# Grouped-query attention in a two-model fp32 kernel: query products and output products inside the attention steps, and the queries' root as the scale of the exponential

## What is computed

```python
def gqa_q(a, g_q, cos, sin, rope):
    q = rms_norm_2(a.reshape(B, T, GQA_HEADS, GQA_HEAD_DIM), g_q)
    if rope:
        q = apply_rope(q, cos, sin)
    return q.reshape(B, T, GQA_KV_HEADS, GQA_GROUP, GQA_HEAD_DIM)

def gqa_mixer(hc, hl, w_in, g_q, g_k, w_out, cos, sin, need_ctx):   # need_ctx is False here
    pl = hl @ w_in
    ql = gqa_q(pl[..., :GQA_Q_W], g_q, cos, sin, True)
    kl, vl = gqa_kv(pl[..., GQA_Q_W:], g_k, cos, sin, True)
    kc, vc = gqa_kv(hc @ w_in[:, GQA_Q_W:], g_k, cos, sin, False)
    return attention(ql, concat([kc, kl]), concat([vc, vl])) @ w_out
```

## Time and profile before

| | |
|---|---|
| device time, median of 3 runs | 1780.71 us (1779.12, 1780.71, 1784.82) |
| span of the profiled execution, first to last instruction | 1781.2 us |
| mean granted TensorE clock in it | 0.986 |
| PE busy | 1684.7 us (95%) |
| DVE busy | 1225.2 us (69%) |
| ACT busy | 917.5 us (52%) |
| granted clock and GB/s, in tenths | one slice of 40 below 9, in the region of 840 to 940 us |

### The profile page before, as it was taken

The page is one execution under the profiler, slowest core; times in us unless marked ns, Lnnn a source line. Parts: engine busy times, 40 slices in busy tenths (PEclk is TensorE's granted clock), DMA queues, the critical chain, the costliest instruction groups (busy, mean ns, idle before and its releaser), DMA issues.

```text
span 1781.2 us, 25178 instructions
## 1 busy us (share of the span) xinstructions
PE 1684.7 (95%) x9916; PEld 1429.3 (80%) x9916; DVE 1225.2 (69%) x1479; ACT 917.5 (52%) x1184; POOL 0.2 (0%) x4
## 2 busy tenths in 40 slices
PE   7979999999998999999989899999999989999998
PEld 5857888988876888889765768888888867789997
DVE  6955778777875778666577359776567655677754
ACT  6475664464437665467457353331233264665552
POOL 0000000000000000000000000000000000000000
PEclk9999999999999999999989999999999999999999
DMA  7913557745651456633140216446644422145551
GB/s 252 299 49 95 163 186 258 238 152 193 201 166 49 148 189 225 213 102 121 38 136 1 67 55 211 154 134 223 221 147 157 162 70 87 39 130 188 187 181 58
DMA packets 240470, 264.75 MB, mean 149 GB/s; under 512 B 7007, under 2 KB 218978, under 8 KB 240354
## 3 DMA queue, kind: packets, MB, share of 16 engines
q1 hardware_dynamic: 238428, 258.84, 44.5%
q10 hardware_dynamic: 1926, 4.32, 0.7%
HBM read 262.08 MB, written 1.05 MB: 148 GB/s over the span
## 4 chain that ended last, share of the span: by engine, by line
PE 76%; ACT 11%; DVE 10%; issue 2%; DMA 0%; ACTq 0%; DVEq 0%
PE ps L718 75%; ACT whi L1191 2%; DVE wlo L1796 2%; ACT y L1579 1%; DVE pr L2332 1%; ACT u L1582 1%; DVE small L2321 1%; DVE y L2082 1%; ACT pr L1727 1%; PE ps L1122 1%; ACT u L1370 0%; ACT sbl L1688 0%; ACT sbe L1684 0%; ACT sbt L1682 0%; DVE rstd L1986 0%
## 5 line engine op out<-in xcount | busy, mean ns | idle before, releaser
L718 PE MATMUL ps<-u,whi 128*128 128x512 f32 (+1 forms) x3472 | 895.5, 341 | 22.8 <-DVE u L2143 5.8
L718 PEld LDWEIGHTS ps<-u,whi 128*128 128x128 f32 x3472 | 596.7, 190 | 117.5 <-issue 16.4
L718 PE MATMUL ps<-u,wlo 128*128 128x256 f32 (+1 forms) x2116 | 648.7, 307 | 0.0
L1796 DVE TENSOR_TENSOR wlo<-raw,whi 128x2048 fp32r<-128x2048 f32 (+6 forms) x212 | 454.0, 2141 | 207.4 <-ACT whi L1191 199.5
L1191 ACT ACTIVATE whi<-raw 128x2048 fp32r<-128x2048 f32 (+6 forms) x212 | 380.7, 1796 | 221.2 <-PE ps L718 202.7
L718 PEld LDWEIGHTS ps<-u,wlo 128*128 128x128 f32 x2116 | 402.2, 190 | 19.6
L718 PE MATMUL ps<-hid,whi 128*128 128x512 f32 (+1 forms) x1212 | 353.6, 363 | 0.0
L718 PE MATMUL ps<-hid,wlo 128*128 128x256 f32 (+1 forms) x864 | 261.9, 303 | 0.0
L718 PEld LDWEIGHTS ps<-hid,whi 128*128 128x128 f32 x1212 | 216.2, 189 | 40.0 <-issue 3.4
L718 PEld LDWEIGHTS ps<-hid,wlo 128*128 128x128 f32 x864 | 163.5, 189 | 7.0
L2082 DVE SCALAR_TENSOR_TENSOR y<-idle_half,cc,y 128x1024 f32<-128x1024 f32 x70 | 89.9, 1285 | 4.9
(11 more groups left out here) (264 smaller groups left out, 1628.9 us busy)
## 6 DMA issues: line engine op xcount, KB each, us to landing
raw<-in_ffn_w_up SPq DMA_DIRECT2D x44, 1024.0 KB, 5.1
raw<-in_w_ff_in SPq DMA_DIRECT2D x32, 1024.0 KB, 5.3
raw<-in_w_ff_out SPq DMA_DIRECT2D x32, 1024.0 KB, 5.0
modw<-in_w_mod SPq DMA_DIRECT2D x112, 256.0 KB, 4.1
idle_half<-in_w_mod SPq DMA_DIRECT2D x80, 256.0 KB, 3.4
raw<-in_w_in_dil SPq DMA_DIRECT2D x18, 1024.0 KB, 5.2
raw<-in_w_in_sb SPq DMA_DIRECT2D x12, 1024.0 KB, 7.9
raw<-in_w_ple_gate SPq DMA_DIRECT2D x8, 1024.0 KB, 4.9
```

What stands on the lines that cost most here:

```text
L718: return pe.matmul(out_, lhsT, rhs, start=start, stop=stop, skip_group_check=True)
L1796: nc.vector.tensor_tensor(wlo[:, s % SPLIT, 0:n], raw[:, c["r"] % RAW, 0:n], whi[:, s % SPLIT, 0:n].bitcast(F32), ALU.subtract).then_inc(* ...
```

## The change

The query job is cut in two: groups 0 and 1 stay ahead of `gqa_v`, and groups 2 and 3 (`gqa_q2`, "merged") get no phase of their own on any engine. Their products, their sums and swaps, and the first two groups of `gqa_out` are issued by hand inside the 16 attention steps. The scores' four banks become two (2 and 3), the transposes' two become one (4); the scores of unit n+1 are issued at the start of step n instead of four units ahead. The queries are no longer multiplied by their root: their sums of squares are taken for each query row (four products with `sq` as weights and 4 columns of ones), the root is a column of `small`, and it becomes the scale of the exponential (ACT) and of the negative maximum (DVE). The wait for the rotated keys ahead of query group 0 goes away, since the keys have banks of their own. `gqa_out` reads its operand from the other half of `u`.

```diff
-                linear("gqa_q", Wi, 8, pairs(0, D), S, "qg")
+                linear("gqa_q", Wi, 8, pairs(0, 512), S, "qg")
                 linear("gqa_v", Wi, 8, pairs(D + 256, 256), T2, "v", mode="V")
+                linear("gqa_q2", Wi, 8, pairs(512, 512), S, "qg")
+                phases[-1].update(merged=True, g0=2)
                 phase("softmax", what="gqa")
-                linear("gqa_out", A["gqa_w_out_2"][0], 8, pairs(0, D), S, "gated")
+                linear("gqa_out", A["gqa_w_out_2"][0], 8, pairs(0, D), S, "gated", tok0=S)
...
-            if p["kind"] != "linear" or phases[p["i"] + 1]["kind"] in ("linear", "final", "dump", "cnorm"):
+            if p["kind"] != "linear" or p.get("merged") or phases[p["i"] + 1]["kind"] in ("linear", "final", "dump", "cnorm"):
                 return [], []
...
-                    if swaps[0] >= 2:
-                        pe.wait_ge(*at("rotated", swaps[0] - (1 if q["evac"] == "qg" and g == 0 else 2)))
+                    if swaps[0] >= 2 and q["evac"] not in ("qg", "kg"):
+                        pe.wait_ge(*at("rotated", swaps[0] - 2))
...
-                            last = mm(ps[:, 6 + swaps[0] % 2, :], ones, sq[:, g % 2, :], True, True)
+                            G = g + q.get("g0", 0)
+                            if G:
+                                pe.wait_ge(*at("rstd_ready", ("head", swaps[0] - 1)))
+                            for t in range(4):
+                                last = mm(head_sums(G)[:, 4 * t:4 * t + 4], sq[:, G % 2, t * P:(t + 1) * P], ones[:, 0:4], True, True)
...
+                                if t == 1 and p["name"] == "gqa_v":
+                                    gqa_scores(p["i"] + 2, 0)
+                                    gqa_scores(p["i"] + 2, 1)
...
+            def gqa_pe(p):
+                def turn(n):
+                    pe.wait_ge(*at("weights_normed", (i, n)))
+                    if n < 1:
+                        pe.wait_ge(*at("group_read_s", ("group", value["gi"])))
+                    else:
+                        pe.wait_ge(*at("turned_copied", (i, n - 1)))
...
+                ahead = {10: (0, 1), 11: (1, 2), 12: (2, 4), 13: (4, 5), 14: (5, 6)}
+                for n in range(16):
+                    if 1 <= n < 15:
+                        gqa_scores(i, n + 1)
+                    if n < 8:
+                        query_products(query, n // 4, n % 4 * 4, n % 4 * 4 + 2)
+                    if n >= 1:
+                        attend(n - 1)
+                    if n < 8:
+                        query_products(query, n // 4, n % 4 * 4 + 2, n % 4 * 4 + 4)
+                    if n in ahead:
+                        out_ahead(out_, 0, *ahead[n])
+                    if n in (4, 8):
+                        pending.append((query, n // 4 - 1))
+                        swap_pending()
+                    turn(n)
+                attend(15)
...
+            def gqa_act(p):
+                for n in range(16):
+                    if n in (4, 8):
+                        evac(query, query["groups"][n // 4 - 1])
+                        pending.append((query, n // 4 - 1))
+                    if n in (5, 9):
+                        head_rstd_pending()
+                    if n < 15:
+                        gqa_exp(i, n + 1)
+                    copy_(n)
+                    if n in (6, 7):
+                        split_high_half(out_["groups"][1][0]["s"], n - 6)
+                    if n in (11, 12):
+                        split_high_half(out_["groups"][2][0]["s"], n - 11)
+                    if n % 2 == 1 and n >= 3:
+                        high_((n - 3) // 2)
+                high_(7)
...
+            def gqa_dve(p):
+                for n in range(16):
+                    if 1 <= n < 15:
+                        gqa_max(i, n + 1)
+                    norm_(n)
+                    if n in (5, 9):
+                        pending.append((query, n // 4 - 1))
+                        rotate_pending()
+                    if n in (7, 8):
+                        split_low_half(out_["groups"][1][0]["s"], n - 7)
+                    if n in (12, 13):
+                        split_low_half(out_["groups"][2][0]["s"], n - 12)
+                    if n % 2 == 1 and n >= 3:
+                        low_((n - 3) // 2)
+                low_(7)
...
-                    if q["evac"] in ("qg", "kg"):
+                    if q["evac"] == "kg":
                         dve.wait_ge(*at("rstd_ready", ("head", swaps[0])))
...
+                        if p["name"] == "gqa_v":
+                            gqa_max(i + 2, 0)
+                            gqa_max(i + 2, 1)
```

More of the change, by code:

```diff
@@ new lines, in out_ahead @@
+            def out_ahead(p, g, k0, k1):
+                c, i = p["groups"][g][0], p["i"] - 1
+                if k0 == 0:
+                    pe.wait_ge(*at("weights_low", c["s"]))
+                    if g == 0:
+                        pe.wait_ge(*at("rotated", query_swaps[3]))
+                    else:
+                        pe.wait_ge(*at("weights_exp", (i, 15)))
+                for k in range(k0, k1):
+                    pe.wait_ge(*at("operand_low", (i, k)))
+                    for j in range(2):
+                        w = [b[:, c["s"] % SPLIT, k * c["C"] + j * P:k * c["C"] + (j + 1) * P] for b in (whi, wlo)]
+                        bank = ps[:, base_bank(c) + j, :]
+                        mm(bank.rearrange("p (h c) -> p h c", h=2), w[0], both(p, k), k == 0, False)
+                        last = mm(bank[:, 0:S], w[1], operand(p, k, S, True), False, k == KD - 1)
+                if k1 == KD:
+                    last.then_inc(*up("weights_used", c["s"]))
@@ L982, in _ @@
                 kind, i = p["kind"], p["i"]
-                if kind not in ("linear", "cnorm"):
+                if kind not in ("linear", "cnorm") and p.get("what") != "gqa":
                     swap_pending()
-                if kind in ("stick", "softmax"):
+                if kind == "stick" or p.get("what") in ("dil", "mla"):
                     last_linear(i)
+                elif kind == "softmax":
+                    pass
                 elif kind not in ("apply", "join", "scale", "entry", "cnorm"):
@@ L1019, in _ @@
                         entry_pe(p)
-                    elif p["evac"] != "ple":
+                    elif p["evac"] != "ple" and not p.get("merged"):
                         linear_pe(p)
+                elif kind == "softmax" and p["what"] == "gqa":
+                    gqa_pe(p)
                 elif kind == "stick":
@@ L1143, in _ @@
                     M = N // heads_of
-                    ahead = dict(mla=2, dil=1, gqa=4)[p["what"]]
+                    ahead = dict(mla=2, dil=1)[p["what"]]
                     for m in range(ahead):
@@ L1147, in _ @@
                     for m in range(M):
-                        if p["what"] != "gqa" and m + ahead < M:
+                        if m + ahead < M:
                             scores(m + ahead)
@@ L1151, in _ @@
                             turn(u)
-                        if p["what"] == "gqa" and m + ahead < M:
-                            scores(m + ahead)
                         if m >= 1:
@@ L1192, in split_high, with split_high_half @@
                     *up("weights_high", s))
+            def split_high_half(s, half):
+                c = splits[s]
+                n = c["kn"] * c["C"] // 2
+                sl = slice(half * n, (half + 1) * n)
+                if half == 0:
+                    act.wait_ge(landed[c["r"] % RAW], 16 * (c["r"] // RAW + 1))
+                    act.wait_ge(*at("weights_used", s - SPLIT))
+                act.wait_ge(*own())
+                nc.scalar.activation(whi[:, s % SPLIT, sl], raw[:, c["r"] % RAW, sl], ACT.Copy).then_inc(*up("weights_high", s if half else (s, 0)))
             def hidden_high(p, g):
@@ L1518, in _ @@
                     act.wait_ge(sem, value)
+                if p.get("merged"):
+                    C.end("scalar", i)
+                    continue
                 for dst, src in p.get("loads", ()):
@@ L1710, in _ @@
                     high(HEADS // 2 - 1)
+                elif kind == "softmax" and p["what"] == "gqa":
+                    gqa_act(p)
                 elif kind == "softmax":
@@ L2298, in _ @@
                     low(HEADS // 2 - 1)
+                elif kind == "softmax" and p["what"] == "gqa":
+                    gqa_dve(p)
                 elif kind == "softmax":
```

179 lines of the change are left out of this document (156 added, 23 removed).

## The result

| | before | after |
|---|---|---|
| device time, median | 1781.78 us (4 runs, 1779.12 to 1784.82) | 1794.91 us (4 runs, 1792.95 to 1803.09) |
| ratio, 95% interval | | 1.0086 (1.0057 to 1.0114) |
| span of the profiled execution | 1781.2 us | 1791.2 us |
| mean granted clock in it | 0.986 | 0.985 |

The change made the kernel slower by 0.9%, 15 us by the ratio. To see where, the two traces are laid over each other from PE's sums of squares of the keys to the product that sums the statistics ahead of the feed-forward part, **the layer** from here on: 1459.34 to 1570.27 before, 110.9 us, and 1456.75 to 1580.06 after, 123.3 us. That is 12.4 us more. The spans differ by only 10.0, because the part ahead of the layer, whose code is the same, came out 2.6 us shorter in this execution.

A forecast was written before the change was run, and what follows sets the result against it. The prediction took PE, busy 95% of the span, as the bound. Added 19.85 us less 0.2, removed 11.4, then 2.5 and 0.3 at the exit gave +11.0, 1791.7 us; range 1787 to 1796.

The forecast's parts named there:

- later norm: Exit: DVE owes work for three output groups, its last split ends behind group 3's products, delaying the norm: +2.5 us.
- The removed stall: Ahead of query group 0's sums: the keys' own banks remove a PE gap and its slow clock, -5.7 us.
- Squares: Queries' sums of squares: four narrow fp32 products replace each wide one, 0.10 us per record, 0.2 us won.
- First transposes: Attention entry: output group 0's split on ACT and DVE delays the norm; PE stands 5.0 us, plus 2.7 of slow clock.
- n = 6 and 8: PE idles 0.5 us in step 6 and 2.05 in step 8, there for query group 3's evacuation; 1.7 slow clock follows.
- Steps 9 to 14: Fresh scores, maximum, norm and odd steps' operands outlast PE's own work: 5.8 us of PE idle time.
- The exit: After the last values: other heads of groups 0 and 1 cover head 7's operands, 0; later norm +2.5 us, dummies and clock 0.3.
- The clock: Slow clock: 2.7 us at the first transposes, 1.7 in step 8, 0.3 for dummies and exit, less 2.8 removed.
- Rival D: Gaps of steps 8 to 14 and 15 add up to more half clock, up to the feed-forward part: some 4 us more, 1796; 15%.
- A: Rival, attention entry: the split does not hold the first transposes, ACT and DVE being ahead; +3.3 us, 1784; 10%.
- C: Rival: PE's own stream decides throughout, transposes ready by 1485.7 and within each step; -7.4 us, 1773; 7%.
- B: Rival: entry stall stays, but maximum and norm overlap PE's work in steps 8 to 15 as before; +1.3 us, 1782; 8%.

The follow-up runs named there:

- e6: Kernel before, one wait weakened: query group 0's sums of squares wait for the keys' roots, not their rotation; ratio to before 0.9968.
- e1: Changed kernel, output group 0's split moved from the values' job in halves into attention steps 1 to 3; ratio to before 1.0055.
- e8: Changed kernel, ten dummy products fill PE's gap ahead of the first transposes, the wait itself stays; ratio to before 1.0095.
- e9: Changed kernel, DVE norms unit n ahead of the maximum of unit n+1 in each attention step; ratio to before 1.0098.
- e3: Changed kernel, second half split of output group 1 moved from ACT's step 7 to 9 and DVE's 8 to 10; ratio to before 1.0079.
- e4: Changed kernel, output group 2 gets banks 6 and 7 and no longer waits for group 0's evacuation; ratio to before 1.0094.
- e10: e9 with PE also taking the value products of unit n-2 in step n instead of n-1; ratio to before 1.0071.
- e13: Changed kernel, behind the attention output group 0 is finished ahead of most of group 1; ratio to before 1.0091.
- e2: Changed kernel, step n issues the scores of unit n+2 behind its value products instead of n+1 at its start; ratio to before 1.0083.
- c1: Changed kernel with the edits of e1, e3, e9 and e10 together; ratio to before 1.0022.
- c2: c1 with all half splits of output groups 1 and 2 moved to other steps in place of e3's move; ratio to before 1.0017.
- c3: c2 with e13's order of output groups added; ratio to before 1.0006.

## Why the prediction was right and wrong

The direction, the main places and the likeliest chance (slower) were right. The time was off: 15.3 us (the ratio times 1781.78) where 11.0 was said, at the upper end of the range. The interval of the ratio is wide, 10 to 20 us, and the layer in the two traces is 12.4 us longer. Term by term, in the traces:

| term | said, us | in the traces, us |
|---|---|---|
| gap ahead of the first transposes | 5.0 | 4.8 |
| slow clock behind it | 2.7 | 2.0 |
| gaps in steps 6 and 8 | 2.55 | 2.4 |
| slow clock in step 8 | 1.7 | 1.7 |
| gaps in steps 9 to 14 | 5.8 | 4.5 |
| gaps in step 15 and at the last values | 1.7 | 1.5 |
| seam, groups 0 to 2: gap and slow clock | 0 | 1.8 and 1.7 |
| later norm (gap ahead of the statistics' product) | 2.5 | 0 |
| removed from the kernel before | -11.4 | -9.8 |
| all else | 0.5 | 1.8 |
| sum | 11.05 | 12.4 |

"All else" is 0.4 for restarts, -0.2 for the squares and 0.3 for dummies and clock at the exit in the prediction, and what is neither a listed gap nor slow clock in the traces. The sum is nearer than its terms deserve: steps 9 to 14 and the removed part were both put too high and partly cancel, and the seam's 3.5 us stand against 2.5 at another place.

**The removed stall**: 5.7 said, 5.7 to 5.9 measured (e6). **Squares**: 0.10 us for each narrow record, as the row said. The Trainium skill's floor (TensorE: Matmul & The Clock Gate, Back-to-back issue gap), by which eight would take an estimated 0.2 us, is not borne out for these: 0.81 us again. **First transposes**: 5.0 said, 4.82 and 4.98 measured (gap and e1), and the cause was the named one. Its slow clock was put at 2.7, from bounds of 1.7 to 2.9, and cost 1.9 here (e1 and e8). Behind the same gap of 4.82 us it cost 1.7 in e9 and 2.6 to 2.8 in e3, e4, e10 and e13, so the bounds were right. **n = 6 and 8**: 0.5 and 2.05 said, 0.53 and 1.84 measured. The 1.7 of clock stood (3.70 us at 0.55 are 1.7 us lost).

**Steps 9 to 14**: the sum "9 1.1, 10 1.5, 11 0.35, 12 1.4, 13 0.35, 14 1.1" stands against gaps of 0.80, 1.38, none listed, 1.41, none listed and 0.90. Its pattern, even and odd, held. What the prediction had not seen is that the chain hung on two queues: with DVE's order mended the same wait appears on ACT (e9).

**The exit**: the step that failed is "the seam is filled: head 6 of group 0 and heads 0 to 6 of group 1 cover head 7's operands, 0". Head 7 is covered, but group 2 needs group 0's banks, and group 0 now ends last. PE waited 1.76 us and ran slow behind it, which lost 1.7 us of its work. "Now it ends 2.5 us behind them: +2.5 on the norm" named the right engine: in the trace DVE's last evacuation follows its split at 1577.03 without delay, but only because PE had been held before; with PE let go, the gap at the end is 3.06, 2.06 more (e4). It is one cost, which shows ahead of group 2 or behind group 3. The prediction took it as fixed; e13 shows that 3.0 us at the exit came from the order in which groups 0 and 1 are finished.

**The clock** is the second term that was mis-sized. It was 2.7 + 1.7 + 0.3 - 2.8, +1.9 us; in the layer of the two traces it is 5.4 - 3.0, +2.4, the piece behind group 2's first product being the one left out. Of the 4.3 us between 15.3 and 11.0 the traces thus show 1.4. The other 3 us are in the timed runs alone, no trace shows where, and the interval of the ratio covers them.

Their mean clocks point to more slow clock, but don't show it. The missing share of the clock times the span is 28.3 us in the mean of the four runs after the change, and 20.6 in 58 runs of the kernel before in the four later batches. That is no cost yet. The mean also counts stretches in which PE stands idle (the gap ahead of the first transposes has 0.70 in it). Also, among those 58 runs, compared within their batches, a run with 1 us more of missing clock is longer by only about 0.5 us. By that price the 7.7 us of difference are worth an estimated 3.7. The batches differ as well: the runs of before beside the result are 3.4 us slower in the mean than the 58, and their clocks are not on record. Rival D had said some 4 us more through slow clock, in the steps from 8 on. In size the 15 us are nearer to it than to the forecast. Its place was wrong in the changed kernel's trace, since steps 9 to 15 ran at 1.00; but e1's trace has just such a stretch at steps 14 and 15. Which share of the 15 us is D's stays open.

Rivals A and C (first transposes not held, PE deciding throughout) fell with the 4.82 us; B fell with the steps of 3.3 to 5.4 us after n = 7.

## What to carry to other kernels

Before filling one engine's idle time with another stage's work, write down for each in-order queue what the moved instructions now stand ahead of; here the split in front of a 0.65 us norm, the maximum in front of a norm, and an exponential in front of a copy cost more than the holes that were filled. When groups share the exit with a slower engine, finish the first group early: its evacuation chain, not the products, sets the end. And look for the smallest edit that removes the known stall; one weakened wait gave 5.7 us, and the rebuilt schedule of which it was a part took 15.

## What the runs showed that was not expected

- The same gap of 1.76 us ahead of group 2 was followed by slow clock in three traces (after, e2, c1) and by 1.00 in six (e1, e3, e8, e9, e10, c2). This window of e1, with PE's columns alone (us, PE busy, PEclk, DMA, GB/s), stands for the six:

```profile
1565.00:1566.00 1.00, 1.00 (x6) 1.00 0.00 0
```

  In the twelve traces of the changed kernel and its variants the layer has 27 gaps of 1.75 to 2.03 us: 12 were followed by slow clock, 15 were not. In step 8 it was seven of nine. Behind the gaps of 2.86 us and more in the layer the clock was always 0.50 for some microseconds; behind single gaps of up to 1.64 us it stayed at 1.00, but for the stretch in e1 behind 0.90 and 0.74. A gap near 1.8 us is thus a chance of losing mostly 1.7 us of PE's work (3.4 once), not a fixed price, and where DVE is the bound, as at the exit, 0.7 to 0.8 of them reach the time. That fits that single runs of one kernel differ by up to 13 us. The part ahead of the layer, the same in all kernels, ended between 1453.8 and 1462.6 us.
- The exponential became dearer with the root as its scale operand. Groups by line in the steps of the changed kernel (1489 to 1551 us):

```profile
L1655 ACT ACTIVATE pr<-ps,small 128x512 f32<-128x512 f32 x14 | 10.9, 778 | 14.3 <-DVE small L2150 13.8
...
L2150 DVE TENSOR_SCALAR small<-small 128x1 f32<-128x1 f32 x14 | 3.0, 214 | 0.5
```

  778 ns in place of 687 in the kernel before, and 214 for the negative, which now takes two factors (the root's column and -1), in place of 153. The Trainium skill (ScalarE: Activation LUTs, What ACT_TABLE_LOAD costs) states about 93 ns for each pointer operand of one column; the 91 ns here agree.
- Open: c3's layer is 2.0 us shorter than before's in the traces, 1.3 of it by less slow clock, but its timed runs are level with it. Two us lie outside of what one trace of each can tell.
